# A float32 block chain on one core: x brought a second time by feature for the first block's products

## What is computed

```
def rms_norm(x, g):
    xf = x.astype(jnp.float32)
    y = xf * lax.rsqrt(jnp.mean(xf * xf, axis=-1, keepdims=True) + RMS_EPS)
    return (y * g.astype(jnp.float32)).astype(x.dtype)

def swiglu(x, w_gate, w_up, w_down):
    return (jax.nn.silu(x @ w_gate) * (x @ w_up)) @ w_down
...
        f1 = swiglu(rms_norm(x, ffn1_pre_g[l]), ffn1_w_gate[l], ffn1_w_up[l], ffn1_w_down[l])
        x = x + FFN_RESIDUAL_WEIGHT * rms_norm(f1, ffn1_post_g[l])
        m = token_mixer(rms_norm(x, mix_pre_g[l]), w_in[l], ...)
        x = x + rms_norm(m, mix_post_g[l])
        f2 = swiglu(rms_norm(x, ffn2_pre_g[l]), ffn2_w_gate[l], ffn2_w_up[l], ffn2_w_down[l])
        x = x + FFN_RESIDUAL_WEIGHT * rms_norm(f2, ffn2_post_g[l])
```

## Time and profile before

| what | value |
|---|---|
| median of 3 runs | 990.95 us (990.85 to 991.25) |
| the profiled execution's own time | 993.97 us |
| its span, first to last instruction | 992.2 us |
| TensorE busy | 987.2 us (100% of the span as the page rounds it) |
| VectorE, ScalarE, GpSimd busy | 71%, 49%, 22% |
| read from memory | 176.89 MB |

### The profile page before, as it was taken

The page is one execution under the profiler, slowest core; times in us unless marked ns, Lnnn a source line. Parts: engine busy times, 40 slices in busy tenths (PEclk is TensorE's granted clock), DMA queues, the critical chain, the costliest instruction groups (busy, mean ns, idle before and its releaser), DMA issues.

```text
span 992.2 us, 14561 instructions
## 1 busy us (share of the span) xinstructions
PE 987.2 (100%) x5318; PEld 832.7 (84%) x5318; DVE 707.7 (71%) x837; ACT 485.3 (49%) x619; POOL 214.6 (22%) x218
## 2 busy tenths in 40 slices
PE   9999999999999999999999999999999999999998
PEld 6888888888878888888888888888888888888887
DVE  5866767765787767676867998677876767666664
ACT  6534444663665533434555444466555445334342
POOL 2322323016100222222111600060000012223230
PEclk9999999999999999999999999999999999999999
DMA  9655556845243555555645525544536356555551
GB/s 297 234 185 178 203 177 205 287 127 193 96 160 127 193 186 201 177 201 185 237 143 193 197 102 197 188 145 149 169 115 224 129 186 232 171 179 199 178 207 42
DMA packets 121017, 178.55 MB, mean 180 GB/s; under 512 B 5764, under 2 KB 82100, under 8 KB 120848
## 3 DMA queue, kind: packets, MB, share of 16 engines
q1 hardware_dynamic: 120048, 174.86, 52.5%
q0 software_dynamic: 576, 1.40, 0.5%
q10 hardware_dynamic: 352, 1.73, 0.5%
HBM read 176.89 MB, written 2.65 MB: 181 GB/s over the span
## 4 chain that ended last, share of the span: by engine, by line
PE 98%; DVE 1%; DMA 0%; ACT 0%; issue 0%
PE acc L687 10%; PE acc L691 10%; PE acc L690 10%; PE tp L888 10%; PE gu L888 10%; PE gu L893 5%; PE tp L893 5%; PE tp L687 4%; PE tp L691 4%; PE tp L690 4%; PE gu L687 3%; PE gu L690 3%; PE gu L691 3%; PE acc L1182 2%; PE acc L1185 1%; PE acc L1211 1%
## 5 line engine op out<-in xcount | busy, mean ns | idle before, releaser
L2048 DVE TENSOR_TENSOR wlo<-raw,whi 128x2048 fp32r<-128x2048 f32 x140 | 326.0, 2334 | 153.5 <-ACT whi L1401 152.0
L1401 ACT ACTIVATE whi<-raw 128x2048 fp32r<-128x2048 f32 x150 | 285.7, 1908 | 69.3 <-PE acc L691 20.4
L888 PE MATMUL tp<-act_in,whi 128*128 128x512 f32 x432 | 102.9, 390 | 0.0
L888 PE MATMUL gu<-act_in,whi 128*128 128x512 f32 x432 | 102.6, 390 | 0.0
L1942 POOL TENSOR_TENSOR tmp<-tmp 128x256 f32<-128x256 f32 x54 | 39.8, 737 | 278.7 <-DVE tmp L2186 278.7
L1944 POOL TENSOR_TENSOR sil<-sil,tmp 128x256 f32<-128x256 f32 x54 | 88.6, 1641 | 33.7 <-ACT sil L1472 33.7
L888 PEld LDWEIGHTS gu<-act_in,whi 128*128 128x128 f32 x432 | 80.9, 188 | 16.6
L687 PE MATMUL acc<-whi,hT_hi 128*128 128x512 f32 x240 | 94.0, 392 | 0.0
L690 PE MATMUL acc<-wlo,hT_hi 128*128 128x512 f32 x240 | 93.7, 390 | 0.0
L691 PE MATMUL acc<-whi,hT_lo 128*128 128x512 f32 x240 | 93.4, 389 | 0.0
L888 PEld LDWEIGHTS tp<-act_in,whi 128*128 128x128 f32 x432 | 79.8, 188 | 15.7
(11 more groups left out here) (395 smaller groups left out, 1837.5 us busy)
## 6 DMA issues: line engine op xcount, KB each, us to landing
raw<-in_w_in SPq DMA_DIRECT2D x96, 512.0 KB, 4.6
raw<-in_down SPq DMA_DIRECT2D x66, 512.0 KB, 4.1
raw<-in_gate SPq DMA_DIRECT2D x62, 512.0 KB, 4.2
raw<-in_up SPq DMA_DIRECT2D x62, 512.0 KB, 4.7
raw<-in_w_out SPq DMA_DIRECT2D x16, 512.0 KB, 4.7
raw<-in_w_branch_hg SPq DMA_DIRECT2D x8, 512.0 KB, 4.3
raw<-in_w_branch_attn SPq DMA_DIRECT2D x8, 512.0 KB, 4.8
post<-in_post_gains SPq DMA_DIRECT2D x3, 512.0 KB, 6.4
```

What stands on the lines that cost most here:

```text
L888: pe.matmul(banks[:, a, :], w_hi[:, i, a * P:(a + 1) * P], both, start=i == 0, stop=False)
L1401: act.activation(split_weights(k)[0], raw_place(k), ACT.Copy).then_inc(hi_ready, 1)
L2048: dve.tensor_tensor(w_lo, raw_place(k), w_hi.bitcast(F32), ALU.subtract).then_inc(lo_ready, 1)
```

## The change

The host passes x once more, laid out by feature: `x_turned`, 128 partitions by 8 k tiles by 256 tokens. SP loads it in four parts of two k tiles (`turned_part`) in the places where the four parts of x stood, into the space of `xs`, which is not used before the first block's end. The first block's x is scaled and rounded from there, k tile by k tile for all 256 tokens at once (`first_turned`, `first_rest`), and no transpose of the first block is left. The products go by k tile: both token tiles of a k tile, then the next, but for the last two, where token tile 0 is finished first. x by token is still needed, for the square sums and the residual: it now comes as two DMAs of 512 KB behind piece 2 and ahead of the rest of `fixed`. The first square sum stands behind `hi(2)` on ScalarE, where it stood between the halves of piece 1. Two more warm-up products stand ahead of the row product and one fewer behind it, and the row product goes through `tp`. The counters of later turns are shifted by the four that are gone (`turn_n`, `scaled_n`).

```diff
-            def x_part(t, h):
-                sp.dma_start(x[:, t, h * BLK:(h + 1) * BLK], x_d[t * P:(t + 1) * P, h * BLK:(h + 1) * BLK])\
-                  .then_inc(x_in[2 * t + h], 16)
+            def x_tile(t):
+                sp.dma_start(x[:, t, :], x_d[t * P:(t + 1) * P, :]).then_inc(x_in[t], 16)
+
+            def turned_part(i):
+
+                sp.dma_start(x_turned[:, 2 * i:2 * i + 2, :], x_turned_d[:, 2 * i:2 * i + 2, :]).then_inc(turned_in[i], 16)
...
             def first_pieces():
-                x_part(0, 0)
-                half_piece(0, 0)
-                x_part(1, 0)
-                half_piece(0, 1)
-                x_part(0, 1)
-                half_piece(1, 0)
-                x_part(1, 1)
-                half_piece(1, 1)
+                for j in range(2):
+                    for a in range(2):
+                        turned_part(2 * j + a)
+                        half_piece(j, a)
...
                 gate_or_up(wg_d[f], n0 + 2, 0, 1)
                 if f == 0:
+                    for t in range(TT):
+                        x_tile(t)
                     sp.dma_start(fixed[:, G_END + P:], fixed_d[:, G_END + P:]).then_inc(fixed_in, 16)
                 gate_or_up(wu_d[f], n0 + 3, 0, 1)
...
                 pe.wait_ge(warm_ready, 1)
-                warm_up(7)
-                pe.wait_ge(head_in, 16)
-                turn(0)
-                warm_up(3)
+                warm_up(9)
                 pe.wait_ge(bias_parts_in, 16)
-                pe.matmul(gu[0:8, 1, 0:S], rel, hot, start=True, stop=True).then_inc(row_product, 1)
+                pe.matmul(tp[0:8, 0, 0:S], rel, hot, start=True, stop=True).then_inc(row_product, 1)
+                warm_up(2)
+                for a in range(4):
+                    pe.wait_ge(tile_lo, 1 + a)
+                    if a < 3:
+                        pe.wait_ge(part_hi, 1 + a)
+                        product(0, 0, a, rests=(part_lo, 1 + a))
+                    else:
+                        pe.wait_ge(hi_ready, 1)
+                        product(0, 0, a, rests=(lo_ready, 1))
+                    mm = product(0, 1, a)
+                mm.then_inc(piece_used, 1)
+                pe.wait_ge(part_hi, 4)
                 for a in range(2):
...
+                    pe.wait_ge(tile_lo, 5 + a)
+                    product(1, 0, a, rests=None if a else (part_lo, 4))
+                    product(1, 1, a)
                 pe.wait_ge(hi_ready, 2)
+                pe.wait_ge(tile_lo, 8)
                 product(1, 0, 2, rests=(lo_ready, 2))
                 product(1, 0, 3).then_inc(gu_first, 1)
...
+                pe.wait_ge(row_copied, 1)
+                product(1, 1, 2)
+                product(1, 1, 3).then_inc(piece_used, 1)
...
+            def first_turned(*tiles):
+
+                for k in tiles:
+                    act.wait_ge(turned_in[k // 2], 16)
+                    act.activation(act_hi[:, k, :], x_turned[:, k, :], ACT.Copy, scale=first_gain(k)).then_inc(tile_hi, 1)
...
+            act.wait_ge(head_in, 16)
+            for a in range(4):
+                first_turned(a)
+                first_hi(0, a, 1)
+                if a == 1:
+                    row_from_bank()
+            first_turned(4, 5)
             first_hi(1, 0, 2)
-            fills(T_FFN1, 2)
+            first_turned(6, 7)
+            first_hi(1, 2, 2)
+            hi(2)
+            act.wait_ge(piece_used, 1)
             x_sums(0, 0)
-            first_hi(1, 2, 2)
-            fills(T_FFN1, 3)
-            hi(2)
             ffn(0, N_FFN1, N_WIN)
...
-    arrays = {"x": of("x", S, D)}
+    arrays = {"x": of("x", S, D), "x_turned": np.ascontiguousarray(of("x", S, KT, P).transpose(2, 1, 0))}
```

More of the change, by code:

```diff
@@ L224, in heads @@
             return ap.rearrange("p (h n) -> p h n", h=n)
-        x_in = [sem(f"x_in{i}") for i in range(2 * TT)]
+        x_in = [sem(f"x_in{t}") for t in range(TT)]
+        turned_in = [sem(f"turned_in{i}") for i in range(KT // 2)]
         part_in = [sem(f"part_in{i}") for i in range(4)]
-        tile_turned, tile_hi, tile_lo = sem("tile_turned"), sem("tile_hi"), sem("tile_lo")
+        tile_hi, tile_lo = sem("tile_hi"), sem("tile_lo")
         part_hi, part_lo, warm_ready, fixed_in = sem("part_hi"), sem("part_lo"), sem("warm_ready"), sem("fixed_in")
@@ L428, in rows_joined, with first_gain @@
             return banks.rearrange("p two (a m) -> p a two m", m=64)
[L430 to L441, removed]
+        x_turned = xs[:, :, :].rearrange("p t d -> p (t d)").rearrange("p (k n) -> p k n", k=KT)
+        def first_gain(k):
+            at = G_TURN + 8 * T_FFN1 + k
             return cols[:, at:at + 1]
         def scaled_n(f):
-            return f - 1
+            return f + 1
         def turned_place(u, t, h):
@@ L469, in turn_n @@
         def turn_n(u):
-            return 4 * u - (4 if u > T_WAT else 0) - (2 if u > T_WOUT else 0)
+            return 4 * (u - 1) - (4 if u > T_WAT else 0) - (2 if u > T_WOUT else 0)
         def stationary(u, t, j, a):
@@ L738, in fill @@
                 f = turn_n(u) + i
-                if f >= 4:
+                if f >= 2:
                     pe.wait_ge(turn_scaled, scaled_n(f - 2))
@@ L767, in first_block @@
                 u = T_FFN1
[L769 to L781, removed]
                 def product(j, t, a, rests=None):
@@ L805, in first_block @@
[L805 to L818, removed]
@@ L2506, in first_lo, with first_rest @@
                    .then_inc(lo_ready if a + n == 4 else part_lo, 1)
-            def first_rest(i, *tiles):
-                for a in tiles:
-                    if a == 3:
-                        dve.wait_ge(act_hi_ready, i + 1)
-                    else:
-                        dve.wait_ge(tile_hi, 3 * i + a + 1)
-                    hi, rest = first_place(i, a)
-                    ins = dve.scalar_tensor_tensor(out=rest, in0=first_bank(i, a), scalar=first_gain(i, a),
-                                                   in1=hi.bitcast(F32), op0=ALU.mult, op1=ALU.subtract)
-                    ins.then_inc(act_lo_ready if a == 3 else tile_lo, 1)
+            def first_rest(*tiles):
+                for k in tiles:
+                    dve.wait_ge(tile_hi, k + 1)
+                    dve.scalar_tensor_tensor(out=act_lo[:, k, :], in0=x_turned[:, k, :], scalar=first_gain(k),
+                                             in1=act_hi[:, k, :].bitcast(F32), op0=ALU.mult, op1=ALU.subtract)\
+                       .then_inc(tile_lo, 1)
             def first_setup():
@@ L2535, in _ @@
             dve.memset(proj[0:8, 0, S:TOEP], MASKED).then_inc(row_padded, 1)
-            first_rest(0, 0)
-            first_lo(0, 0, 1)
-            first_rest(0, 1)
-            first_lo(0, 1, 1)
-            first_rest(1, 0, 1)
-            first_rest(0, 2, 3)
-            first_rest(1, 2, 3)
-            first_lo(0, 2, 1)
-            first_lo(0, 3, 1)
-            fill_scaled(T_FFN1, 2)
+            dve.wait_ge(head_in, 16)
+            for a in range(4):
+                first_rest(a)
+                first_lo(0, a, 1)
+            first_rest(4, 5)
             first_lo(1, 0, 2)
-            fill_rest(T_FFN1, 2)
-            fill_scaled(T_FFN1, 3)
+            first_rest(6, 7)
             first_lo(1, 2, 2)
-            fill_rest(T_FFN1, 3)
             lo(2)
@@ L2918 @@
     row = nc.dram_tensor("bias_rows", (8, TOEP), F32, kind="Internal").ap()
-    build(nc, d["x"], [d[f"gate{f}"] for f in range(3)], [d[f"up{f}"] for f in range(3)],
+    build(nc, d["x"], d["x_turned"], [d[f"gate{f}"] for f in range(3)], [d[f"up{f}"] for f in range(3)],
           [d[f"down{f}"] for f in range(3)], d["w_in"], d["w_out"], d["w_in_2"], d["w_branch_hg_2"],
```

39 lines of the change are left out of this document (3 added, 36 removed).

## The result

The changed kernel takes 994.09 us (median of 7, 993.9 to 995.83) against 991.12 us before (median of 7, 990.84 to 991.25): ratio 1.0036, interval 1.0026 to 1.0046. It is slower by 3.0 us, and the prediction (990.8, range 989.8 to 993.2) is wrong.

The account below looks back on a forecast made before the run. TensorE was taken as the bound; its gain of 2 to 4.5 us is eaten by a wait of 1.9 to 4.4 us for piece 3, leaving 0.1: 990.95 - 0.1 = 990.8 us, range 989.8 to 993.2.

Parts of the forecast that it names:

- the sum: Up products: piece 3 at 24.1 plus hi(3), hand-over, lo(3) and first product gives 28.6, against 28.71 before; gain 0.1 us.
- Turns gone, x by feature: Opening: sixteen transposes leave TensorE, products begin at about 7.1 not 8.3, pieces 0 to 2 land as before.
- ScalarE's order: Opening on ScalarE: moved square sum keeps hi(3) from starting before 23.5; as the deciding rival 990.2 us, chance 0.18.
- Piece 3's landing: DMA queue ahead of the up products: 1.05 MB more puts the landing at 24.1; it decides, 990.8 us, chance 0.60.
- The clock's fall: Rival at the up products: the new wait returns TensorE to 1.2 GHz, losing 1.7 to 3.4 us; 993.4 us, chance 0.16.
- the first rival: Opening: new bytes fill the DMA hole, ScalarE's order decides, hi(3) at 23.5, gain 0.75 us; 990.2 us, chance 0.18.
- in full: Rival at the up products: TensorE's earlier arrival passes on, 2 to 4.5 us gained; 987.7 us, chance 0.06.
- What is late next: Down products: piece 4's hidden tile is ready at T + 9.0, needed at T + 10.0 (T = piece 3's landing); nothing lost.

Follow-up runs that it names:

- e5: The kernel before, unchanged, run again for a second trace: 991.24 us; the execution traced took 991.58 us.
- e12: The changed kernel, unchanged, run again for a trace near its median: 994.13 us, ratio 1.003.
- e1: The changed kernel with 12 products of 512 columns on TensorE in its wait ahead of the up products: 994.39 us.
- e2: The changed kernel with 6 products of 512 columns on TensorE in its wait ahead of the up products: 994.09 us.
- e8: Changed kernel with x by token behind piece 4, square sums from x by feature ahead of hi(2), eleven products on zeros in place of nine: 991.41 us.
- e11: Changed kernel with x by token and rest of `fixed` behind piece 4, square sums from x by feature ahead of hi(2), eleven products on zeros: 990.81 us.
- e4: The changed kernel with x by token behind piece 4 and both square sums taken from x by feature ahead of hi(2): 991.54 us, ratio 0.9996.
- e7: The changed kernel with x by token behind piece 4, square sums from x by feature at their places in the changed order: 995.67 us, ratio 1.0047.
- e3: The kernel before with 1 MB more (x by token once more) in SP's queue behind piece 2: 993.51 us.
- e9: Changed kernel with x by token behind piece 4, square sums from x by feature in changed order, VectorE's lo(2) in four parts: 993.46 us.

## Why the prediction was wrong

**The step that failed** is the comparison in the sum, "Before: 28.71", with "the differences are put on the median". The forecast of the moment itself came near: piece 3 at 24.1 (measured 24.2), up products at 28.6 (28.80), a wait of 1.9 to 4.4 us (2.66), spacing behind it unchanged in most executions. But 28.71 belongs to an execution of 993.97 us. In e5, an execution of 991.58 us, these products begin at 26.24. With the forecast's own 28.6 and 965.3 us for what follows, the sum gives 993.9; 994.09 was measured. The sign was lost not in the change but in the baseline.

The hint was there to be read: the profiled execution was 3.0 us above the median of the three runs and 2.7 above the longest, and the earlier trace rows showed 7.4 us of work at the low level. The prediction prices just that stretch at 3.4 us, for a rival, and does not ask whether the 3 us between trace and median were this. It treats the excess as 0.3% of the whole.

**Turns gone, x by feature.** Predicted: products from about 7.1, pieces 0 to 2 land as before. Measured: 7.79, and piece 2 at 16.62 against 16.15 in the trace that the prediction read and 15.91 in e5. The first part of x lands at 5.2 to 5.5 us in the nine traces with x by feature, at 4.0 to 5.0 in the five by token, same size and place in the queue; what follows is later with it. The constants on ScalarE's queue, which are the same in both kernels, are as late (5.4 to 5.7 us against 4.3 to 5.2), so it is not that transfer alone. The cause stays open. In e5 the kernel before reaches its gate products at 20.13, in e12 the changed one at 19.79, and in e1 and e2, with the same opening, at 20.55 and 20.42: what the turns give TensorE with this opening is no more than 0.5 us in any trace, not 2 to 4.5. With the clock up from the first product, as in e5, it is 0.95 to 1.1 (e8, 19.18; e11, 19.04).

**ScalarE's order.** Predicted: `hi(3)` not before 23.5. Measured: 24.52, 1.0 us later. Of that, 0.4 is piece 2's later landing: the square sum begins at 18.47, not 18.06. Another 0.8 is GpSimd: from the start of the square sum to the end of the power it is 3.1 us (18.47 to 21.59 in the chain), where the prediction had 2.29 from another place. The second tile's chain gave 0.2 back (21.98 to 24.52, in place of 2.72). Against e5 (21.27) it is 3.25 us later: `hi(2)` begins 0.70 later (16.64, 15.94); from there to the first Silu it is 4.97 us (16.64 to 21.61) in place of 1.82 (15.94 to 17.76), since the first square sum and its norm now stand between; from Silu to Silu 2.53 in place of 3.13. 0.70 + 3.15 - 0.60 = 3.25. The prediction saw the moved square sum and found it covered by piece 3's landing, which it missed by 0.3 us (24.52 against 24.2), and all but covered by the 23.24 of a late execution, where a typical one has 21.27.

**Piece 3's landing.** Right, 24.2 against 24.1, with two small errors that cancel: without the megabyte piece 3 lands at 21.7 in the changed kernel (e4, e7), not at 21.3, and the megabyte costs 2.5 us, not 2.7 to 3.0. In the sum, too, luck helped: `hi(3)` was 0.4 us later than its 24.1, as ScalarE's order and not the landing ended last, and TensorE began 0.06 us behind `lo(3)`, not 0.23. Either limit alone holds the up products: the landing to 28.05 (e3, in the kernel before), the order to 28.68 (e7). Removing the landing alone gains 0.1 us, removing both gives the 2.7 us back (e4).

**The rivals.** The clock's fall exists and costs 1.7 us where it comes, the lower end of its price, but on top of the loss. ScalarE's order did end last, as the first rival has it, but at 24.52 and not at 23.5, and so without a gain. The order and the landing did shut out "in full", and there was less to pass on than 2 to 4.5 us: with both out of the way (e11) the up products are 1.1 us earlier than in e5. In e5 `lo(3)` ends at 23.20 + 2.29 = 25.49, so with its order and landing no more than 0.75 us could have been passed on.

**What is late next.** Piece 4 did not become a second wait, as predicted: in e12 the down products follow the up products without a wait.

## What to carry to other kernels

Before subtracting a trace's moment from a median, ask where the profiled execution's own excess lies; if it lies in the stage that the change touches, take the moment from a trace of a typical execution, or subtract the excess first (here 26.2 by the one and 25.7 by the other, not 28.71). A work item that is moved behind another takes its whole chain along (square sum, a small GpSimd operation, a power, a Silu), and each link is priced with what runs beside it at the new place. Where two limits end within a few tenths of a microsecond, test each alone and then both: removing one of them may show almost nothing, as in e7.

## What was unexpected of the hardware

**GpSimd stands behind VectorE.** In the changed kernel (trace of 994.13 us) VectorE's `lo(2)` and GpSimd's first operation on 128x1 end together:

```profile
18.59 2.29 DVE L2009 TENSOR_TENSOR wlo<-raw,whi 128x2048 fp32r<-128x2048 f32 x1 [2.62 <-ACT whi L1371]
```

```profile
19.69 1.24 POOL L1886 TENSOR_SCALAR ms<-sums 128x1 f32<-128x1 f32 x1 [3.24 <-ACT junk L1392]
```

18.59 + 2.29 = 20.88 and 19.69 + 1.24 = 20.93. It is the same in e5, where the operation starts later in the subtraction and takes 0.81:

```profile
17.89 2.29 DVE L2048 TENSOR_TENSOR wlo<-raw,whi 128x2048 fp32r<-128x2048 f32 x1 [0.97 <-ACT whi L1401]
```

```profile
19.42 0.81 POOL L1925 TENSOR_SCALAR ms<-sums 128x1 f32<-128x1 f32 x1 [2.07 <-ACT junk L1423]
```

17.89 + 2.29 = 20.18 and 19.42 + 0.81 = 20.23. With the subtraction in quarters (e9) it takes 0.25. The Trainium skill, "SBUF — State Buffer", section "SBUF: two separate sides", states that VectorE operations with two inputs in SBUF and GpSimd operations that read it share a port pair which one of them holds for a whole instruction; these rows agree.

**The clock's moment is not fixed by the kernel.** The same kernel before worked at the 1.2 GHz level to 12.5 us in one execution and was at the 2.4 GHz level before 9 in another. A wait of 2.66 us (e12) left the level up. Behind waits of 2.68 (e7) and 2.77 it fell, 1.3 to 1.5 us after the work had begun again. Behind 0.64, 1.13 and 1.43 it stayed up: in these runs the length alone does not tell. In the openings of e1, e2 and e9 the level was up by 6 us, fell at about 8.4 us behind pauses of no more than 0.95 us, and was back at 11.5 to 12 us.
